# Gates' scratch by key column groups, a stage's first weights in two passes, and down products that wait tile by tile

## What is computed

```python
# PEER: 8 heads, 16 picks each out of 128 x 128 experts, for every token
q = rms_norm(h, g) @ w_query                     # 16 projections of 128
s1, s2 = top 16 of q1 @ keys1, top 16 of q2 @ keys2
picks, gates = top 16 of s1 + s2, softmax
y = sum over picks of gate * gelu(h @ u[expert]) * v[expert]

def hybrid_layer(x):                             # twice
    x = x + 0.5 * (silu(n1(x) @ w_gate) * (n1(x) @ w_up)) @ w_down    # ffn1
    x = x + mixers(norm(x) @ w_in) @ w_out
    x = x + 0.5 * (silu(n2(x) @ w_gate) * (n2(x) @ w_up)) @ w_down    # ffn2
    return x
```

## Time and profile before

| | us |
|---|---|
| three executions | 3990.87, 4002.89, 4026.34 |
| median | 4002.89 |
| the profiled execution | 4013.38 |
| its span | 4012.1 |
| PE busy | 3762.7 (94%) |
| DVE busy | 2311.8 (58%) |
| ACT busy | 1347.9 (34%) |
| POOL busy | 577.3 (14%) |
| gates store, 12 x 2048 KB, median to landing | 10.8 |
| gates back, 32 x 768 KB, median to landing | 9.5 |

### The profile page before, as it was taken

One profiled execution on the slowest core, in us unless ns is written; L12 is line 12 of the kernel. 1 busy time (PEld: TensorE's weight loads), 2 busy tenths in 40 slices (PEclk: granted clock), 3 DMA queues, 4 the chain that ended last, 5 costly groups with the idle time before them and its releaser, 6 DMA issues. The chain is left out here.

```text
span 4012.1 us, 46391 instructions
## 1 busy us (share of the span) xinstructions
PE 3762.7 (94%) x18298; PEld 3106.7 (77%) x18298; DVE 2311.8 (58%) x4014; ACT 1347.9 (34%) x2352; POOL 577.3 (14%) x610
## 2 busy tenths in 40 slices
PE   9879999999899999899999789999999999699999
PEld 7767999888877777788777557887887877467877
DVE  5746899888678887633257754332433267843332
ACT  3354333344333333422233333222322143243221
POOL 8500012322434444000000100000000000100000
PEclk9679999999999999999999789999999999699999
DMA  3003368888999999533322102233222221012222
GB/s 124 11 11 95 113 214 298 289 303 310 356 329 347 342 345 339 169 95 95 95 69 74 34 1 90 95 95 100 79 94 96 95 69 53 19 48 79 95 95 74
DMA packets 273433, 574.70 MB, mean 143 GB/s; under 512 B 19952, under 2 KB 159376, under 8 KB 271552
## 3 DMA queue, kind: packets, MB, share of 16 engines
q1 hardware_dynamic: 236256, 437.42, 33.2%
q0 software_dynamic: 36864, 134.23, 9.1%
q10 hardware_dynamic: 96, 0.08, 0.0%
HBM read 517.92 MB, written 53.74 MB: 142 GB/s over the span
## 5 line engine op out<-in xcount | busy, mean ns | idle before, releaser
L348 DVE TENSOR_TENSOR wlast<-wraw,wlast 128x1024 fp32r<-128x1024 f32 x406 | 494.9, 1224 | 510.7 <-ACT wlast L338 510.3
L357 PE MATMUL ps<-XH,wlast 128*128 128x512 f32 (+2 forms) x1888 | 721.9, 382 | 10.3 <-ACT arena L2039 10.3
L359 PE MATMUL ps<-XH,wlast 128*128 128x512 f32 (+2 forms) x1888 | 706.7, 374 | 0.0
L358 PE MATMUL ps<-XL,wlast 128*128 128x512 f32 (+2 forms) x1888 | 706.7, 374 | 0.0
L338 ACT ACTIVATE wlast<-wraw 128x1024 fp32r<-128x1024 f32 x406 | 424.8, 1051 | 247.6 <-PE ps L359 233.1
L348 DVE TENSOR_TENSOR wtwo<-wraw,wtwo 128x1024 fp32r<-128x1024 f32 x212 | 259.5, 1226 | 290.8 <-ACT wtwo L338 290.4
L357 PEld LDWEIGHTS ps<-XH,wlast 128*128 128x128 f32 x1888 | 357.1, 189 | 70.5 <-ACT arena L2039 10.9
L359 PEld LDWEIGHTS ps<-XH,wlast 128*128 128x128 f32 x1888 | 356.7, 189 | 55.7
L358 PEld LDWEIGHTS ps<-XL,wlast 128*128 128x128 f32 x1888 | 357.7, 189 | 54.0
L357 PE MATMUL ps<-XH,wtwo 128*128 128x512 f32 (+1 forms) x960 | 368.1, 383 | 0.0
L358 PE MATMUL ps<-XL,wtwo 128*128 128x512 f32 (+1 forms) x960 | 361.9, 377 | 0.0
(11 more groups left out here) (500 smaller groups left out, 6836.8 us busy)
## 6 DMA issues: line engine op xcount, KB each, us to landing
wraw<-in_ut SPq DMA_DIRECT2D x128, 512.0 KB, 4.9
wraw<-in_v SPq DMA_DIRECT2D x128, 512.0 KB, 6.9
wraw<-in_ffn_gate SPq DMA_DIRECT2D x88, 512.0 KB, 3.5
wraw<-in_ffn_up SPq DMA_DIRECT2D x88, 512.0 KB, 3.4
wraw<-in_ffn_down SPq DMA_DIRECT2D x88, 512.0 KB, 3.4
wraw<-in_w_in SPq DMA_DIRECT2D x58, 512.0 KB, 3.6
acts<-arena SPq DMA_DIRECT2D x128, 192.0 KB, 5.1
gates<-arena SPq DMA_DIRECT2D x12, 2048.0 KB, 10.8
```

What stands on the lines that cost most here:

```text
L348: ve.e.tensor_tensor(W.items[n][8], W.rawof(n), W.items[n][7], ALU.subtract).then_inc(*ve.up("wlo", n))
L357: mm(out, lh, rh, start=start, stop=False)
L358: mm(out, lh, rl, start=False, stop=False)
L359: return mm(out, ll, rh, start=False, stop=stop)
```

## The change

Three things change.

1. **The gates' scratch.** In DRAM it was [group g of 32 tokens][partition][128 key columns x 32 tokens]. Now it is [4 key columns][partition][group g][4 x 32]. A store was 128 rows of 16 KB; it is now 128 x 32 pieces of 512 bytes. Reading back was 128 x 12 pieces of 512 bytes; it is now 128 rows of 6 KB.
2. **The first projection of a stage** (`pe_opening`) runs over three token tiles (384 columns) first; after the fifth of its eight column blocks comes the turn of the fourth tile; then the other three, then all eight blocks again over the fourth tile alone (128 columns). The turned fourth tile lies in six banks instead of eight. The turn no longer stands at the end of the stage before. So that the fourth tile is the first or the last in memory, the order of tiles from Peer to the first Ffn is 3, 1, 2, 0 where it was 3, 0, 1, 2, and Peer's last matmuls follow it.
3. **Down products** wait for HL of their own block, not for the last one, and each bank is opened when its first product comes, from the bank after that of the last `up`.

```diff
+def pe_opening(k, key, norm, XH, XL, lo=0, hi=8):
+    pe, at, n = k.pe, k.at, norm.n
+    early, late = norm.order[2], norm.order[3]
+    wide, narrow = (slice(0, 384), slice(384, 512)) if late == 3 else (slice(128, 512), slice(0, 128))
+    wh, wl, m = k.W.pair(key)
+    pe.wait_ge(*at("wlo", m))
+    for j in range(8):
+        if j % 4 == 0:
+            pe.wait_ge(*at("xLt", n, early, j // 4))
+        if j == 0:
+            o = k.open(lo, hi, key)
+        three(k, o[:, wide], wh[:, j, :], wl[:, j, :], XH[:, j, wide], XL[:, j, wide], j == 0, j == 7)
+        if j == 4:
+            norm.pe_turn(late, k.bank[key,] + 1)
+    for j in range(8):
+        pe.wait_ge(*at("xL", n, j))
+        last = three(k, o[:, narrow], wh[:, j, :], wl[:, j, :], XH[:, j, narrow], XL[:, j, narrow], j == 0, j == 7)
+    last.then_inc(*pe.up("proj", key))
...
-        self.next.pe_turn(3)
...
-        self.gd = k.nc.dram_tensor("gates", (DENSE * 4, 128, 128 * 32), F).ap()
+        self.gd = k.nc.dram_tensor("gates", (32, 128, DENSE * 4, 128), F).ap()
...
-                    sp.e.dma_start(self.gd[g], self.GS[g % 2].rearrange("p j t -> p (j t)")).then_inc(
+                    sp.e.dma_start(self.gd[:, :, g, :].rearrange("c p n -> p c n"),
+                                   self.GS[g % 2].rearrange("p (c j) t -> p c (j t)", j=4)).then_inc(
...
-        src = self.gd[:, :, 128 * c:128 * c + 128].rearrange("g p n -> p g n")
-        sp.e.dma_start(self.GC[c % 2].rearrange("p g j t -> p g (j t)"), src).then_inc(
+        sp.e.dma_start(self.GC[c % 2].rearrange("p g j t -> p (g j t)"),
+                       self.gd[c].rearrange("p g n -> p (g n)")).then_inc(
...
-        ps = {}
-        for m in range(4):
-            for n in range(2):
+        ps, last_up = {}, k.bank[(*id, "up", 21),]
+
+        def one(f, m, n, w):
+            if f == 0:
                 ps[m, n] = k.open(2 * m + n, 2 * m + n + 1, "down", *id, m, n)
...
-        pe.wait_ge(*at("hl", *id, 21))
+        first = (last_up + 1) // 2
         for f in range(self.TAIL):
             w = k.W.pair((*id, "down", f))
             pe.wait_ge(*at("wlo", w[2]))
-            for m in range(4):
+            pe.wait_ge(*at("hl", *id, f))
+            for m in [(first + i) % 4 for i in range(4)]:
```

More of the change, by code:

```diff
@@ L546, in __init__, with place, pe_turn @@
         self.D = [mem[:, 128 * i:128 * i + 128] for i in range(4)]
-    def pe_turn(self, i):
+    def place(self, i, j):
+        if i != self.order[3]:
+            return j // 4, 128 * (j % 4)
+        return (j, 0) if j < 4 else (2 + j // 2, 128 * (j % 2))
+    def pe_turn(self, i, after=None):
         k, n, pe, at = self.k, self.n, self.k.pe, self.k.at
@@ L552, in pe_turn @@
         for j in range(8):
[L554 to L557, removed]
+            g, c = self.place(i, j)
+            if c == 0:
+                b = (after + 1 + g) % 8 if single else 2 * i + g
+                o = k.open(b, b + 1, "xT", n, i, g)
             pe.e.matmul(o[:, c:c + 128], k.X[:, i, j * 128:(j + 1) * 128], self.D[i], start=True,
@@ L580, in ac_upper @@
         for j in js:
-            ac.wait_ge(*at("xT", n, i, "column", j if i == self.order[3] else js[-1]))
+            ac.wait_ge(*at("xT", n, i, "column", (j if j < 4 else j | 1) if i == self.order[3] else js[-1]))
             ac.e.activation(self.XH[:, j, 128 * i:128 * i + 128], self.source(i, j), ACT.Copy,
@@ L607, in ve_lower @@
             if single:
-                last.then_inc(*ve.free(("xT", n, i, j)))
+                last.then_inc(*ve.free(("xT", n, i, self.place(i, j)[0])))
                 ve.note("xL", n, j)
@@ L1964, in pe_u @@
             if kind == "wq":
-                pe_proj(k, (kind, c), self.XH, self.XL, 0, 4, parts=("xL", 1))
+                if c == 0:
+                    pe_opening(k, (kind, c), self.norm, self.XH, self.XL, 0, 4)
+                else:
+                    pe_proj(k, (kind, c), self.XH, self.XL, 0, 4)
                 if c:
@@ L2343, in pe_v @@
         ws = {j: k.W.pair(("V", j)) for j in range(TAIL, 128)}
-        for i in range(DENSE):
+        for p, i in enumerate(self.next.order[1:]):
             for j, w in ws.items():
@@ L2347, in pe_v @@
                 pe.wait_ge(*at("al", j))
-                if j == 127 and i:
-                    if i == 1:
+                if j == 127 and p:
+                    if p == 1:
                         self.next.pe_turn(self.next.order[0])
-                    self.next.pe_turn(self.next.order[i])
+                    self.next.pe_turn(self.next.order[p])
                 for n in range(2):
@@ L2357, in pe_v @@
             pe.note("wused", w[2])
-        self.next.pe_turn(self.next.order[3])
         k.end("peer", pe)
@@ L2411, in ve_v @@
                 ve.note("x+", "peer", i, n)
-            self.next.ve_tile(1 + i)
+            self.next.ve_tile(1 + p)
         k.end("peer", ve)
@@ L2481, in pe @@
         for f in range(22):
-            pe_proj(k, (*id, "gate", f), self.XH, self.XL, parts=("xL", self.norm_n))
+            if f == 0:
+                pe_opening(k, (*id, "gate", f), self.norm, self.XH, self.XL)
+            else:
+                pe_proj(k, (*id, "gate", f), self.XH, self.XL)
             pe_proj(k, (*id, "up", f), self.XH, self.XL)
-        ps = {}
-        for m in range(4):
-            for n in range(2):
+        ps, last_up = {}, k.bank[(*id, "up", 21),]
+        def one(f, m, n, w):
+            if f == 0:
                 ps[m, n] = k.open(2 * m + n, 2 * m + n + 1, "down", *id, m, n)
-        def one(f, m, n, w):
             a, c = slice(128 * m, 128 * m + 128), slice(512 * n, 512 * n + 512)
@@ L2515, in pe @@
             pe.note("wused", w[2])
-        if self.next:
-            self.next.pe_turn(3)
         k.end(id, pe)
@@ L2848, in pe_proj1 @@
         k, l, XH, XL = self.k, self.l, self.XH, self.XL
-        for m in (0, 2):
-            pe_proj(k, ("cu", l, m), XH, XL, 0, 5, parts=("xL", self.norm_n))
-            yield
+        pe_opening(k, ("cu", l, 0), self.norm, XH, XL, 0, 5)
+        yield
+        pe_proj(k, ("cu", l, 2), XH, XL, 0, 5)
+        yield
         for m in range(2):
@@ L3876, in build @@
         plan_ffn(k, "ffn1", l)
-        stages.append(Ffn(k, "ffn1", l, f"f1{l}", norm, before, (0, 1, 2, 3) if l else (GATHERED, 0, 1, 2)))
+        stages.append(Ffn(k, "ffn1", l, f"f1{l}", norm, before, (0, 1, 2, 3) if l else (GATHERED, 1, 2, 0)))
         plan_mixer(k, l)
```

10 lines of the change are left out of this document (7 added, 3 removed).

## The result

| | before | after |
|---|---|---|
| median of eight executions, us | 4005.6 | 3975.0 |
| range | 3990.9 to 4026.3 | 3962.0 to 3985.3 |
| ratio, 95% interval | | 0.9922 (0.9904 to 0.994) |
| span of the profiled execution | 4012.1 | 3980.5 |

The ratio of 0.9922 is 31 us less (24 to 38), where 37 were forecast; 3975.0 lies in both ranges that the prediction names (3950 to 3985 and 3935 to 4007) and 9 us above the forecast of 3966. In the two profiled spans the gain is 31.6 us. It is made up otherwise than the sum was. The table divides both spans at the same instructions of PE; a gain is positive. The down sequences are taken with the gate and up blocks before them.

The account below looks back on a forecast made before the run. PE, busy 94% of the span, was taken to bound the kernel, V losing where gates' bursts precede acts. Gains 19 + 16 + 2 = 37 gave 3976 for the profiled execution, 3966 as median (3950 to 3985); range 3935 to 4007.

Parts of the forecast that it names:

- V: Peer's V, gates read back 32 times in 6 KB packets: shorter waits behind the gates, 23 us gained of 39 lost.
- stores: Gates stored 12 times as 4096 packets of 512 bytes: 2 us lost over eleven stores, 2 at the twelfth.
- down products: Four down sequences: the 9.5 us wait for HL goes, and 1.6 us of slow clock behind each; 16 us gained.
- starts: Seven stage starts: each 1.2 us sooner, about 0.3 left after an expected slow stretch; 2 us gained in all.
- 604 packets per us: Gates' transfers: rate of 512-byte packets alone, 318 GB/s, set against 450 GB/s in a stretch with 16 KB packets.
- 22 of 40: V: 1.2 us off each of DVE's waits behind the gates, mean 1.75, so 22 of 40 us go.
- Rival 1: V doesn't gain, since the burst shrinks by only 0.8 us and engines stay over 90% busy: 3984 us; chance 0.15.
- rival 3: All of V's loss goes, since waits feed on each other, and starts lose their slow stretch: 3943 us; chance 0.14.
- Rival 4: Gates stores starve beside gathers, under 333 packets per us, so ACT and PE wait: 4019 us at 250; chance 0.12.
- Rival 2: Stage starts: narrow 128-column matmuls cost 0.24 us each instead of 0.112, 21 us worse in all: 3987 us; chance 0.15.
- I expect one in most new starts: Stage starts: a slow-clock stretch, 1.0 us in the old start, stays in most new ones, leaving about 0.3 us gain each.

## Why the forecast was right, and where it was not

**The sum, term by term.** Means over the profiles that share the part in question, so that one execution's luck weighs less:

| term | forecast | the two profiles | means |
|---|---|---|---|
| V | 23 | 20.1 | 587.6 to 571.2: 16.4 |
| stores | -4 | -2.6 | U 732.2 to 733.8: -1.5 |
| down products | 16 | 15.6 | 14.2 |
| starts | 2 | 8.0 | 88.4 to 82.6: 5.8 |
| mixers of the second block | 0 | -9.1 | -7.8 |
| sum | 37 | 31.6 with -0.4 elsewhere | 27.1 |

The means' sum and the timed 31 (24 to 38) agree. The three parts timed alone give 13.6 + 12.0 - 2.4 = 23; each carries some 5 to 7 us of uncertainty, so that they add up to the timed 31 within it. Of the 9 us by which the forecast was too low, 6 are gain that didn't come; 3 are its starting point, since the kernel before has a median of 4005.6 us over eight executions and had 4002.9 over three.

**V.** Right in mechanism, in the mean too large by 6.6 us. The reads' new pattern was the cause: with reads alone changed V is as short. That it is the packets' size, as the forecast had it, is argued from 604 packets per us and not shown apart from their place in DRAM. (The 450 GB/s of its sum come from a stretch that mixes sizes, 152 of 229 packets under 8 KB.) Most signs foretold came: DVE's wait for acts 20.5 us (about 18), PE's for AL 17.9, less than before but not near 14, gates landing in 8.3 (under 9), 833 matmuls (815 or more). Taking "22 of 40" of the waits was near the measured 19.7 of DVE's. 833 matmuls ask for 193 us at the steady rate, so V still loses 7 of 200, some 19 in all, where it lost 39. That is the profiles' 20 us; but the old V varied by itself from 581 to 591 us, and its first profile, on which the 39 rested, was near the upper end. Rival 1 is refuted by 16 us, and rival 3, the whole loss, didn't come even with the transfers halved. The Trainium skill (DMA: Bandwidth & Descriptors, Specifications) would have had no gain from leaving 512-byte packets; V gained 16.4 us in the mean, so the runs speak for the row, unless it is the place in DRAM that paid.

**Stores.** The sizes were near, -1.5 to -2.6 for -4 (no more than U's scatter), but I had overlooked something: SP's own issue. I had counted 2.1 us more of the engines' time per store and asked who waits for the transfers behind. What happens first is that the next load can't be issued for 4.4 us. That is hidden, eleven times, by weights loaded ahead and by the 17 us until ACT needs its buffer. The acts stores still landed in 9.6 us at most before the twelfth, as in the kernel before. At the twelfth, experts follow each other faster, and PE idles 5 to 8 us with the block of 11.0 to 12.8 us even where SP waits for no store, as the kernels with later reads show. The forecast had one idle time of 7 to 12 us there. It was 8.4, in the bounds, and one us shorter than before. Rival 4's rate came true only at the twelfth (291 packets per us beside gathers, against its limit of 333), as the argument against it had it. Its ground, queues that go packet by packet as in 1041:1042, didn't hold there: 2907 packets passed against 569.

**Down products.** Right in every step: the wait gone, the clock at 1.00, no new wait in its place. The lost 1.6 us of the slow stretch were 1.4 (8 matmuls ask for 1.9 of the 3.3 us).

**Starts.** The timeline was right nearly to the tenth: first 384-column product 2.55 us behind the last old one (2.47 forecast), all through after 11.25 (11.4), 24 narrow matmuls in 2.63 us (2.7). Rival 2 is refuted. The step that failed is "I expect one in most new starts". Slow stretches stand in 11 of the 70 new starts of ten profiles, none in the changed kernel's own first one; one costs 1.5 us. So the term is 8 us in a lucky execution and 5.8 in the mean.

**What was not in the sum at all** is the mixers. I had assumed that stretches which no edit touches keep their time. They lost what the starts won and somewhat more. That happens with new starts alone and with new down products alone, and goes with a lower mean clock, not with other work: the instructions of PE are the same 1635. The clock goes with the place at which the mixer begins: the six mixers at 0.8 to 1.3 in the pattern took 387 us, with 89 to 96 us of it at half clock, and the longest, at 1.8, took 399.6 with 116. Kernels with the old starts and the old down products have five of their six mixers there. All the others have one of 22, the one with a repeated step. So the step that failed here is the term of 0, the assumption that a stretch which no edit touches keeps its time. The likely reason is that an edit ahead of it moves its begin, and with it the clock's changes in it. How the place makes the clock fall more or less often, and why mixers at nearly the same place still differ (391.6 and 395.2 at 3.2), is open, and no kernel was run that puts both mixers at 1.1 on purpose. It isn't the opening as such (down products alone do it). The Trainium skill (TensorE: Matmul & The Clock Gate, Part 1) says that the clock's control runs free and doesn't start with the kernel, so that the same program meets it at other places. The repeats of both kernels agree with that much: 387.0 at 1.15 and 390.35 at 2.4 for the same mixer. No kernel that puts short idle times back in front of the mixers was tried.

In the two profiles the misses, +6 and -9 against the term of 2 and the term of 0, nearly cancel. That is luck, and it, not the sum's exactness, is why 3966 came within 9 us.

## What to carry to other kernels

Read the price of a transfer in packets from a stretch of the trace that holds nothing else, count it on both sides of a scratch in DRAM, and look at the issue's own duration on SP: some thousand packets in one transfer block the issue of whatever stands behind. Where a kernel's clock already wanders, a few us taken from one stage may be given back in the next (here the mixers began at other places in the clock's pattern): a gain of that size is believed from timed runs of the part alone, never from the stage's own rows. Before a stretch's change is explained, look how much it varies in a second profile of the same program.

## What the runs showed of the hardware that was not expected

- Behind a transfer of 4096 packets of 512 bytes the issue of the next load mostly takes SP 4.0 to 4.8 us instead of 0.33, and 9.3 to 11.8 when gathers fill the other queue. Behind 2048 packets it takes under 2, once 3.2; behind two such halves 5 us apart, 12.75. In the changed kernel it ends, but for one case, when about 3000 to 3500 of the 4096 packets have begun.
- Beside full gathers SP's queue passed 2907 packets of mostly 512 bytes in 10 us while the gathers passed 569 (2.10 MB): 54 and 53% of the engines' time.
- The mean granted clock of one and the same sequence of 1635 matmuls lies between 0.86 and 0.89, which is 387 to 400 us. Its length goes with the place in the pattern of the clock's changes at which it begins: six of 28 begin at 0.8 to 1.3 us and take 386.7 to 387.0, the others 388.4 to 399.6. In another execution of the same program the sequence took 3.3 us more (387.0, 390.35).
- V, with none of its transfers changed, took 590.4, 590.6, 588.2 and 581.1 us.
